# Hybrid decoder block with a mixture of experts, on one core: a new order for the tail of the first stage and the opening of the experts

## What is computed

```
h = rmsnorm(x); proj = h @ w_in
gla = gated linear attention over q, k, v with decays log_a, normed, * silu(g)
ssd = Mamba-2 state space scan over conv(xbc) with decays dt, * silu(z), normed
x = x + concat(gla, ssd) @ w_out
h2 = rmsnorm(x)
logits = h2 @ router_w + router_b; top 4, gates = softmax(top 4)
for each expert e, over the tokens that picked it:
    gate = min(h2 @ w_gate[e] + b_gate, 7); up = clip(h2 @ w_up[e] + b_up, -7, 7)
    y += gates * (((up + 1) * gate * sigmoid(1.702 * gate)) @ w_down[e] + b_down)
out = rmsnorm(x + y) * final_norm_w
```

## Time and profile before

| | us |
|---|---|
| median of 3 runs | 3581.7 |
| lowest and highest run | 3580.57, 3585.46 |
| the profiled execution, own time | 3587.3 |
| its span in the profile | 3585.3 |
| TensorE busy | 3416.9 (95%) |
| VectorE busy | 2147.9 (60%) |
| ScalarE busy | 1661.4 (46%) |
| GpSimd busy | 613.5 (17%) |

### The profile page before, as it was taken

How to read it: one execution, slowest core, us unless ns; L and a number is a source line. 1 busy time by engine, 2 the same in 40 slices (tenths; PEclk the granted TensorE clock), 3 DMA queues, 4 the chain that set the end, 5 groups by cost and what they waited for, 6 DMA issues and landing times.

```text
span 3585.3 us, 58999 instructions
## 1 busy us (share of the span) xinstructions
PE 3416.9 (95%) x22297; PEld 3159.5 (88%) x22297; DVE 2147.9 (60%) x2762; ACT 1661.4 (46%) x2161; POOL 613.5 (17%) x835
## 2 busy tenths in 40 slices
PE   6999999999984999999999999999999999999993
PEld 5888888888873999999999999988888899999992
DVE  3565345435544555655666666567766777777774
ACT  3443333233331444444444444455555556656664
POOL 1011111111113111111121121112112212212121
PEclk8999999999996999999999999999999999999996
DMA  9888887887854555556666566576667667768776
GB/s 341 333 307 326 306 289 288 299 316 271 295 203 146 171 170 169 170 182 184 185 193 196 180 205 188 170 220 201 213 190 219 209 220 224 220 208 245 234 235 245
DMA packets 474349, 821.53 MB, mean 229 GB/s; under 512 B 19040, under 2 KB 420592, under 8 KB 457856
## 3 DMA queue, kind: packets, MB, share of 16 engines
q1 hardware_dynamic: 442320, 716.52, 57.9%
q0 software_dynamic: 24432, 76.27, 9.2%
q10 hardware_dynamic: 7488, 27.27, 2.1%
HBM read 720.85 MB, written 99.16 MB: 229 GB/s over the span
## 4 chain that ended last, share of the span: by engine, by line
PE 66%; DMA 1%; DVE 1%; ACT 0%; issue 0%; POOL 0%; POOLq 0%; SPq 0%; DVEq 0%; ACTq 0%
PE acc L2234 21%; PE acc L2236 11%; PE acc L2230 10%; PE acc L2231 10%; PE acc L2232 10%; PE tpm L2213 2%; PE tpm L2207 2%; DMA fin<-xacc_d 1%; DMA xacc_d<-ybuf,tabm 0%; DMA xg<-h_d,tab 0%; DMA tab<-tab_d 0%; DVE wlo L1719 0%; ACT squares L1236 0%; DVE fin L1804 0%; ACT ybuf L1187 0%
## 5 line engine op out<-in xcount | busy, mean ns | idle before, releaser
L1719 DVE TENSOR_TENSOR wlo<-raw,whi 128x2048 fp32r<-128x2048 f32 x388 | 888.1, 2289 | 304.4 <-ACT whi L1172 304.4
L2234 PE MATMUL acc<-xhl,whi 128*128 128x512 f32 (+3 forms) x2304 | 771.0, 387 | 2.4 <-ACT ybuf L1187 2.4
L1172 ACT ACTIVATE whi<-raw 128x2048 fp32r<-128x2048 f32 x388 | 741.5, 1911 | 19.7 <-DMA raw<-in_moe_w_gate 18.9
L621 POOL TENSOR_TENSOR gate_op<-gate_op 1x1 f32<-1x1 f32 x346 | 155.9, 450 | 2825.0 <-ACT ybuf L1187 880.8
L2236 PE MATMUL acc<-xhl,wlo 128*128 128x256 f32 (+3 forms) x2304 | 625.7, 272 | 0.0
L2230 PE MATMUL acc<-xhl,whi 128*128 128x272 f32 (+3 forms) x1792 | 536.0, 299 | 9.1 <-DVEq L1774 9.1
L2231 PE MATMUL acc<-xhl,whi 128*128 128x272 f32 (+3 forms) x1792 | 531.3, 296 | 0.0
L2232 PE MATMUL acc<-xhl,wlo 128*128 128x272 f32 (+3 forms) x1792 | 531.1, 296 | 0.0
L2234 PEld LDWEIGHTS acc<-xhl,whi 128*128 128x128 f32 x2304 | 433.4, 188 | 69.8 <-issue 2.6
L2236 PEld LDWEIGHTS acc<-xhl,wlo 128*128 128x128 f32 x2304 | 438.7, 190 | 0.0
L2234 PE MATMUL acc<-ahl,whi 128*128 128x512 f32 (+3 forms) x1152 | 387.7, 388 | 0.0
(11 more groups left out here) (292 smaller groups left out, 5781.1 us busy)
## 6 DMA issues: line engine op xcount, KB each, us to landing
u<-split_d SPq DMA_DIRECT2D x112, 2048.0 KB, 8.9
raw<-in_moe_w_gate SPq DMA_DIRECT2D x130, 1024.0 KB, 5.2
raw<-in_moe_w_up SPq DMA_DIRECT2D x130, 1024.0 KB, 5.0
raw<-in_moe_w_down SPq DMA_DIRECT2D x128, 1024.0 KB, 6.7
split_d<-u SPq DMA_DIRECT2D x16, 2048.0 KB, 10.1
uraw<-in_w_in SPq DMA_DIRECT2D x12, 1024.0 KB, 13.7
fin<-xacc_d SPq DMA_DIRECT2D x4, 2048.0 KB, 14.7
out<-fin SPq DMA_DIRECT2D x16, 512.0 KB, 8.5
```

Source lines behind the costliest of these rows:

```text
L621: pool.tensor_tensor(gate_op[0:1, 0:1], gate_op[0:1, 1:2], gate_op[0:1, 1:2], ALU.add).then_inc(gate_ran, 1)
L1172: act.activation(whi[:, q % RING, :, :], raw[:, q % RING, :, :], ACT.Copy).then_inc(a_hi, 1)
L1719: dve.tensor_tensor(wlo[:, q % RING, :, :], raw[:, q % RING, :, :], whi[:, q % RING, :, :].bitcast(F32), ALU.subtract).then_inc(v_lo, 1)
L2234: pe.matmul(into[:, 0:2 * n].rearrange("p (c n) -> p c n", c=2), hi_, of[:, k, :, 0:n], start=(k == 0), stop=False)
```

## The change

It rewrites the order of the tail on all engines and the opening of the experts.

- TensorE: `half_out` becomes `out_part`, a quarter of a half (6 matmuls), and the 16 parts stand between other steps. The mixed tile 14 is turned before the decays of tile 15.
- VectorE: the SSD state is added before the ramp; tile 14's mixed output is copied and split ahead of q and k. The normalised rows of tiles 12 to 15 are copied into hraw, which the tail leaves free, instead of mT (`last_h2T`, `last_logits`). Five steps of the tiles' table and three copies into tabm stand ahead of the output adds.
- pair, sloti and the semaphore d_slots exist twice, by the parity of the tile: `route` waits for the writes of the tile two before.
- SyncE issues the load of the first table, ahead of the weights, and then two weight units, the biases, and, behind a wait for the second gather, two more. GpSimd begins with the gather.
- The second block of rows is turned into acc instead of tpm. v_e is primed before the first weight split; one weight unit is split ahead of the rows and three behind them.

```diff
-            def route(j):
+            def route(q, t):
+                j = q * 2 + t
                 after(dve, "pe_lg.lg", j)
                 tt(lg[:, :], p_lg, rb_b, ALU.add, R + "lg")
-                if not (isinstance(j, int) and j == 0):
-                    dve.wait_ge(d_slots, j * (16 * TOPK))
+                if not (isinstance(q, int) and q == 0):
+                    dve.wait_ge(d_slots[t], q * (16 * TOPK))
...
             sp.wait_ge(tiles_known, 1)
-            sp.wait_ge(d_slots, 16 * TOPK * TILES)
+            for t in range(2):
+                sp.wait_ge(d_slots[t], 8 * TOPK * TILES)
+            row = sp.value_load(sched[1:2, 0:1], min_val=0, max_val=SLOTS - 3 * P)
+            sp.dma_start(tab[:, :, :], tab_d[bass.ds(row, 3 * P), :].rearrange("(b p) two -> p b two", p=P)).then_inc(d_tab0, 16)
             first = expert_of(sp, 0)
-            for q in range(RING):
+            for q in range(2):
                 load(first, q)
             after(sp, "pe_rk.rank", TILES - 1)
             after(sp, "act_rt.exp", TILES - 1)
             sp.dma_start(mcols[:, :, :].rearrange("p e c -> p (e c)"), moe_cols).then_inc(d_mcols, 16)
+            sp.wait_ge(d_g[1], 16)
+            for q in range(2, RING):
+                load(first, q)
...
-            load_tab(row_of(0))
+            pool.wait_ge(d_tab0, 16)
+            gather(N)
             last = last_chunks(pool)
-            pool.wait_ge(d_tab, 16)
-            gather(N)
...
             sum_sq(z - 2, 1)
-            h2_of(end - 1, 0)
+            mixed_hi(z - 1, 0, end - 1)
             decays(z)
             tok_out(z)
+            h2_of(end - 1, 0)
+            qk_out(z)
             h2_of(end - 1, 1)
-            qk_out(z)
-            mixed_hi(z - 1, 0, end - 1)
...
-            for q in range(2):
-                lo(0, q)
-            for r in range(3):
-                x_evict(0, r, N)
-                x_lo(0, r, N)
-            for q in range(2, RING):
+            dve.drain().then_inc(v_e, PRIMED)
+            lo(0, 0)
+            x_evict(0, 0, N)
+            x_evict(0, 1, N, acc[:, 2, :, :].rearrange("p b n -> p (b n)"))
+            x_lo(0, 0, N)
+            x_evict(0, 2, N)
+            x_lo(0, 1, N)
+            x_lo(0, 2, N)
+            for q in range(1, RING):
                 lo(0, q)
...
-            dve.drain().then_inc(v_e, PRIMED)
...
+            def out_part(t, c, part):
+
+                n = 12 + 2 * c + part // 2
+                q = n % 2
+                if part % 2 == 0:
                     ready(PAIRS, n, PAIRS)
...
+                for k in range(part % 2 * 2, part % 2 * 2 + 2):
+                    for h_, w_ in ((th, wh), (th, wl), (tl, wh)):
...
             state(z - 1)
+            after(pe, "act_tok.tok", z - 1)
+            mixed_turned(z - 1)
             after(pe, "dve_pos.cnt", z - 4)
             decays(z, 1, end)
-            after(pe, "act_tok.tok", z - 1)
+            after(pe, "dve_mt.mT", z - 1)
             cv_turned(1, end)
+            after(pe, "dve_ml.ml", z - 1)
+            after(pe, "dve_x2.b1", end - 1)
+            for part in range(3):
+                out_part(0, 0, part)
             after(pe, "act_rec.eb", z)
             cb_products(1)
             after(pe, "act_tok.tok", z)
             qk_turned(z)
+            out_part(0, 0, 3)
```

More of the change, by code:

```diff
@@ L711, in _ @@
             out_root(end - 3, 1, 70)
-            slots(end - 5, 71)
+            slots(end - 5, 1, 71)
             gla_root(end - 1, 72)
@@ L715, in _ @@
             out_root(end - 2, 0, 74)
-            slots(end - 4, 75)
+            slots(end - 4, 0, 75)
             out_root(end - 1, 1, 76)
-            slots(end - 3, 77)
-            slots(end - 2, 78)
-            slots(end - 1, 79)
-            pool.wait_ge(d_slots, 16 * TOPK * TILES)
+            slots(end - 3, 1, 77)
+            slots(end - 2, 0, 78)
+            slots(end - 1, 1, 79)
+            for t in range(2):
+                pool.wait_ge(d_slots[t], 8 * TOPK * TILES)
             for t in range(2):
@@ L1163, in _ @@
                 act.wait_ge(d_h2[t], 8 * TILES)
-            act.wait_ge(d_slots, 16 * TOPK * TILES)
+            for t in range(2):
+                act.wait_ge(d_slots[t], 8 * TOPK * TILES)
             act.drain().then_inc(a_e, PRIMED)
@@ L1464, in gate, with place @@
                 after(dve, "dve_gate.rs", j)
[L1465 to L1467 removed]
+                done(dve.tensor_scalar(pair[:, t, :, 1], ex[:, :], exs[:, 1:2], None, ALU.mult), "dve_gate.gate")
+            def place(q, t):
+                j = q * 2 + t
                 R = "dve_pos."
@@ L1660, in step @@
                 dve.wait_ge(sched_step, steps[0])
-            after(dve, "dve_pos.cnt", TILES - 1)
+            end, z = PAIRS - 1, TILES - 1
+            mix_ssd(z - 1)
+            ssd_add(z - 1)
+            ramps(z, 1, end)
+            after(dve, "dve_ml.ml", z - 2)
+            mixed_T(z - 1)
+            mixed_lo(z - 1, 0)
+            qkv(z, 1, end)
+            ssd_in(z, 1)
+            masked(z)
+            ssd_y(z, 1, end)
+            last_h2T(z - 3, 0)
+            mix_gla(z, 1, end)
+            mix_ssd(z)
             step(dve.tensor_scalar(sbase[:, :], iot[:, 0:E + 1], float(STRIDE), None, ALU.mult))
@@ L1667, in _ @@
             step(dve.memset(small[:, KINDS - 1:], -1.0))
+            for r in range(3):
+                step(dve.tensor_copy(tabm[:, r, :], spare[:, :]))
+            dve.wait_ge(d_xres[0], end * 16 + 16)
+            after(dve, "pe_oz.a0", 0)
+            add_out(0, 0, "dve_xz.a0", 0)
+            after(dve, "dve_ml.ml", z - 1)
+            mixed_T(z)
+            after(dve, "pe_oz.a1", 0)
+            add_out(0, 1, "dve_xz.a1", 1)
+            mixed_lo(z, 1)
+            last_h2T(z - 2, 1)
+            route(end - 1, 0)
+            gate(end - 1, 0)
+            place(end - 1, 0)
+            dve.wait_ge(d_xres[1], end * 16 + 16)
+            after(dve, "pe_oz.b0", 0)
+            add_out(1, 0, "dve_xz.b0", 0)
+            route(end - 1, 1)
+            gate(end - 1, 1)
+            place(end - 1, 1)
+            last_h2T(z - 1, 0)
+            after(dve, "pe_oz.b1", 0)
+            add_out(1, 1, "dve_xz.b1", 1)
+            route(end, 0)
+            gate(end, 0)
+            place(end, 0)
+            last_h2T(z, 1)
+            route(end, 1)
+            gate(end, 1)
+            place(end, 1)
+            after(dve, "dve_pos.cnt", TILES - 1)
             step(dve.tensor_tensor(cnt1[:, :], cbase[:, :], sbase[:, 0:E], ALU.subtract))
@@ L1712, in _ @@
                 dve.wait_ge(d_h2[t], 8 * TILES)
-            dve.wait_ge(d_slots, 16 * TOPK * TILES)
+            for t in range(2):
+                dve.wait_ge(d_slots[t], 8 * TOPK * TILES)
             dve.memset(yT[:, :, :], 0.0).then_inc(v_zero, 1)
@@ L2162, in _ @@
             gla_out(z, 1, end)
-            after(pe, "dve_mt.mT", z - 1)
             h2_turned(z - 3, 0)
-            after(pe, "dve_ml.ml", z - 1)
-            after(pe, "dve_x2.a1", end - 1)
-            half_out(0, 0)
-            after(pe, "dve_ssd.cbm", z)
-            logits(z - 3)
+            for part in range(3):
+                out_part(0, 1, part)
             after(pe, "dve_th.h2T", z - 3)
             mixed_turned(z)
-            after(pe, "dve_x2.b1", end - 1)
-            half_out(0, 1)
-            after(pe, "dve_rt.lg", z - 3)
-            ranks(z - 3)
+            out_part(0, 1, 3)
+            after(pe, "dve_ssd.cbm", z)
+            last_logits(z - 3, 0)
             after(pe, "dve_mt.mT", z)
@@ L2179, in _ @@
             after(pe, "dve_xz.a0", 0)
-            half_out(1, 0)
+            for part in range(3):
+                out_part(1, 0, part)
+            after(pe, "dve_rt.lg", z - 3)
+            ranks(z - 3)
+            out_part(1, 0, 3)
             after(pe, "dve_pos.cnt", z - 3)
-            logits(z - 2)
+            last_logits(z - 2, 1)
             after(pe, "dve_xz.a1", 0)
-            half_out(1, 1)
+            for part in range(2):
+                out_part(1, 1, part)
             after(pe, "dve_rt.lg", z - 2)
@@ L2188, in _ @@
             h2_turned(z - 1, 0)
+            for part in range(2, 4):
+                out_part(1, 1, part)
             after(pe, "dve_pos.cnt", z - 2)
-            logits(z - 1)
+            last_logits(z - 1, 0)
             after(pe, "dve_rt.lg", z - 1)
@@ L2195, in _ @@
             after(pe, "dve_pos.cnt", z - 1)
-            logits(z)
+            last_logits(z, 1)
             after(pe, "dve_rt.lg", z)
```

148 lines of the change are left out of this document (55 added, 93 removed).

## The result

The changed kernel takes 3550.4 us (median of 4 executions, 3549.23 to 3553.89) where the kernel before takes 3581.1 on the same chip: ratio 0.9914, 95% interval 0.9900 to 0.9929. The medians differ by 30.7 us; 34.6 were forecast. One execution in this study, of the kernel with no load ahead of the gathers, took 4883 us at a mean granted clock of 0.65; it is in no ratio.

A forecast was written before the change was run, and what follows sets the result against it. TensorE, busy 95% of the span, was taken as the bound, with gains only in the seam between first stage and experts. 21.3 us up to T plus 13.3 in the opening make 34.6: 3581.7 to 3547.1 us, own range 3542 to 3552, overall 3539 to 3558.

The forecast's parts named there:

- The gathers gain nothing from fewer weights in flight: Rival on the experts' opening: gathers take as long as before, second 2.3 us later than forecast; result 3549.4 to 3554.3, chance 0.17.
- A: First-stage tail: projection parts fill TensorE's waits at full clock, so the last part ends at 1070.5, not 1081.28; 10.8 us.
- B: Last projection part to the tiles' table: earlier logits 3.3, entry waits 5.2, clock 0.5, steps and copies 1.5 us.
- list of what would show it: Signs for the tail: TensorE without a stand over 1.5 us from 1029 to 1070, clock 1.00, last part ending near 1070.5.
- The clock falls in the tail: Rival: TensorE drops to half clock at 1028 until projection is dense, losing some 9.7 us; result 3557, chance 0.10.
- T: Moment when VectorE's schedule arithmetic for the tiles' table ends; forecast to move 21.3 us, from 1115.84 to 1094.5.
- both waits of the pair copies: VectorE's waits for the entry buffer at tiles 14 and 15: entries by parity remove them, worth 5.2 us.
- The term of 0.5 us for the clock: Ranks of tile 14 and transposes of tile 15: 1.9 us of half-clock work becomes 1.0, 0.3 lost.
- C: Experts' opening: table issued first, two weight loads held back; first product at T+19.9 instead of T+33.2, 13.3 us.
- A table load with little beside it: First table load in the experts' opening: 2.5 us from issue to landing, against 6.4 beside four weight loads.
- the first gather near T+9.5, the second T+12.5: Landing times in the opening, chosen between old bandwidth shares and all of it, with 3.7 MB under way at 360 GB/s.
- sign of being wrong: Opening: the prediction counted itself wrong if, among other signs, the gathers land as late as before.

## Why the prediction was right, point by point

The time forecast was 3547.1, the measured 3550.4, inside the forecast's own range of 3542 to 3552. It lies as well in the range of the rival "The gathers gain nothing from fewer weights in flight", 3549.4 to 3554.3, so the time alone doesn't choose between them; the profile does, piece by piece, and for the gathers it is the rival that holds. That the sum came out right in spite of it rests on A and B, and on a range wide enough for a miss of 2 us.

**A, 10.8 us: right.** 11.1 in the profile. The list of what would show it held: clock 1.00, no stand over 1.5 us. The last part ended at 1071.4, which on the start of before is 1070.2, forecast 1070.5. What I had not said is how far this rests on a store of 512 KB: ScalarE had room for one that lands 7 us after the sums; it landed after 7.9. In the profiles with fillers everywhere and with the table on GpSimd it took 12.2 and 11.9, TensorE stood 2.5 to 2.8 us, and with the fillers the clock fell: my rival "The clock falls in the tail", by another cause than I gave it. The new order covers part of what a late store costs (2.8 us of stand where the old order showed 10.3), but not the clock.

**B, 10.5 us together: right, but its terms are not the worth of the single edits.** T came at 1095.8, on the start of before at 1094.6 (forecast 1094.5). Tile 14's logits are picked up 1.9 us behind the last part instead of 5.3, so 3.4 for the forecast's 3.3; both waits of the pair copies, 5.2, are gone. The term of 0.5 us for the clock was 0.1: the ranks of tile 14 ran at the full clock, but the transposes of tile 15 took 1.67 us at a mean of 0.59, and the two with the gap between them 2.69 us where it was 2.80. What the terms hide is that the buffer and the order need each other. With the new opening, the new order is worth 5.2 us of seam without the second buffer (111.91 less 106.71) and 20.9 with it (111.91 less 90.97). The buffer is worth 15.7 us in the new order and nothing measurable in the old one, where I had read its price.

**C, 13.3 us: 11.35, and this is the step that failed: that fewer weights in flight bring the gathers early.** Two terms were mis-sized. "A table load with little beside it", 2.5 us, was nearly right: 2.8, and 1.9 to 2.8 in the profiles with it on SyncE's queue. But from its landing to the gather's issue I had counted 0.3 us, and it took 0.9 in each of them (0.2 to 0.3 where GpSimd had issued the table itself), so the gather left at T+4.7, not T+3.8. And "the first gather near T+9.5, the second T+12.5", my choice between bandwidth as before and all of it: T+12.7 and T+14.7, with 0.1 us between it and what the rival "The gathers gain nothing from fewer weights in flight" has. The total was right: the DMA engines' rates in the changed kernel from 1095 to 1113 us, 40 slices of 0.45 us, are

```profile
GB/s 0 0 0 0 0 0 21 4 0 166 139 323 360 362 382 382 360 362 348 346 355 339 357 410 414 401 387 389 417 421 405 401 150 53 25 14 0 80 241 357
```

at 339 to 421 from 1100.4 until 1109.4, which is T+13.6, with 13.5 forecast for all of it. But I let the gathers finish ahead of the loads; the first gather and the second load come in together (1108.52 and 1109.14). From their issue the gathers took 8.0 and 8.7 us, where they had taken 7.1 and 9.7: as late as before, which I had named as a sign of being wrong. They come earlier only because they are issued earlier. The second is 2.2 us late, 0.9 of it by its issue and 1.3 by its own length (8.7 us, not the 7.4 of the forecast). Of this 0.2 were made good behind it: from the second gather to the first product it took 7.2 us, not 7.4.

What the opening did gain, 11.35 us, splits by the two profiles into three. The first gather is issued at T+4.7 instead of T+8.6: 3.9 us (with the table back on GpSimd's queue the first product was 2.3 us later). From there to the second gather's landing it is 10.0 us instead of 11.0: 1.0 us. And from there to the first product it is 7.2 us instead of 13.6: 6.4 us, VectorE's new order and the earlier counter. No run makes or undoes that last and largest part alone; it rests on the two profiles.

The Trainium skill ("DMA: Bandwidth & Descriptors", Queues, rings and completion order) says that each DMA engine takes turns, packet by packet, between the queues that it has work for. By that the length of the other queue would not matter, while its being empty would: the runs agree (8.0 us with two loads ahead, 7.7 with four, 4.5 with none). Holding back the third and fourth load, the part of the change that I had credited, is worth 0.85 us; holding back the second, with the biases, 2.55 more in the one profile of it.

**The rest: right.** TensorE has no stand from the first product to 1160 (42.32 of 42.32 us busy), so none at the third unit, the slots' writes held nothing, the experts run as before: 2297.01 of 2300 us at clock 1.00. That the measured gain is 30.7 and the seam's 32.6 is within what the untouched 2430 us vary between executions.

## What to carry to other kernels

When two edits loosen the same chain, one by moving steps closer together and one by doubling a buffer, don't price them one by one from the waits of the old order: the wait of a single buffer can grow with what the new order saves. To get a small indexed transfer early, it is not enough to shorten the queue of large ones beside it; have it empty, or down to what ends before the small one's own data start. And an in-order engine that waits for a store should have all work that others wait for ahead of that wait: two moved lines gave 7 us of seam.

## What the hardware showed that I had not expected

- One and the same store of 512 KB, from the end of ScalarE's sums to its landing, took 7.8 to 12.2 us in profiles of kernels with the same code up to there. It decides whether the tail has a stand. In the changed kernel SyncE issues a weight load of 2 MB at 1026.9, directly ahead of it, and the four such loads around it took 8.0 to 9.7 us to land; why the store is late in some executions, no run here tests.
- SyncE can be held by an issue: with all four loads ahead of the gathers, the fourth load of 1 MB took 5.56 us to issue, and the biases behind it 4.06, where the first takes 0.41. A load listed as queued early may not be so.
- Stands of like length were followed by different clocks. In the changed kernel, after 2.04 us ahead of tile 14's ranks, the next transposes took 1.67 us, partly at half, where 1.04 is full speed, and the logits behind a further 1.47 us took 3.59, where 1.86 is; TensorE had been busy 39.20 of 39.67 us before tile 14's logits. In the kernel before, after 2.27 us at 1028.78 the decays ran at 1.00, and after 1.90 us the logits of tile 14 took 1.95 us at 0.98. And a stand of 2.78 us in the tail was followed by 9.55 us at 0.50, one of 2.53 us at the same place in another kernel by 9.3 us at 1.00.
